# State space projections of a two-block kernel, issued as one stream with gate chunks between input and key blocks

## The chip, the cores and the metric

The kernel runs on one core of a Trainium2 chip. The metric is the device time of one execution in microseconds (us), read as the median over several executions. The core has TensorE (PE, matrix products), VectorE (DVE), ScalarE (ACT), GpSimd (POOL) and SyncE (SP, which here issues the loads of weights). Each engine works through its own instructions in order and waits for others at semaphores.

## The reference, cut to what matters

The program computes two blocks. The first is left as it is. The second has two layers; the first of them (a hybrid mixer) is left as it is as well, and the second is a state space mixer (SSD, both directions) followed by a feed-forward part. What the change touches is the mixer's input:

```
p = modulated(h) @ w_in                   # 1024 -> 2048 + (2048+1024+1024) + 32
z, xbc, dt = split(p)                     # gate z, input x / keys B / queries C, step sizes
x, B, C = silu(dwconv_centred(xbc, w, b)) # 5 taps along the tokens, per feature
dt   = softplus(dt + dt_bias)             # one bias per direction
dta  = dt * -exp(a_log)
y    = scan(x, B, C, dt, dta)  (two directions) + d_skip * x
out  = rmsnorm_by_group(y * silu(z)) @ w_out
```

There are 256 main tokens and 256 context tokens. x and B are needed for all 512 (they build the state), C and z only for the 256 main ones. `dt` is needed for all.

## The kernel before, in words

Weights arrive as 32-bit numbers and are split on chip: ACT writes the high part (`weights_hi`, line 244), DVE the remainder (`weights_lo`, line 251), and every product is three matmuls, hi by hi, hi by lo, lo by hi (`three_products`, lines 300 to 302). A unit is 512 KB of weights, 128 x 1024. There are four buffers for raw units and two for split ones, so ACT may split unit n only when PE has multiplied unit n-2, and SP loads unit n when DVE has split unit n-4.

`modulated_input` (line 2354) normalises the 512 tokens, transposes them and splits them into `work_split` and `input_split`; between its steps it splits the first two weight units (`split_first_weights`, line 2407).

`ssd_mixer` (line 3773) then runs these steps, each ended by a semaphore that all engines wait for:

- `convolution(0, 6, 2)`: six chunks of four units; a unit makes one block of 128 features for 512 tokens (24 matmuls of 512 columns). These are the four chunks of x and the two of B. The bank contents are copied into padded buffers (ACT line 3823, DVE line 3807), DVE applies tap 0 (line 3839) and taps 1 to 4 (line 3841) from the pad, and ACT applies silu with the bias (line 3814). Half of a chunk's taps come after the first half, in `half_taps`, behind a pair of weight splits.
- `convolution(6, 2, 1)`: two chunks of C for 256 tokens (24 matmuls of 256 columns per unit). It starts when the first call has ended.
- `transposes` (line 590): x and B are turned to tokens by rows, 96 transposes on PE in six batches, each batch copied out by ACT and DVE.
- `gemm_token_major` with width 32: dt for four tiles of 128 tokens, 96 matmuls whose moving side has 32 columns.
- `gemm_token_major` with width 512: z for two tiles, four chunks of four units (12 matmuls of 512 columns per unit).
- silu of z (ACT, 3927), exp of a_log (ACT, 3933), d_skip times x (DVE, 3946).
- For each direction: bias, softplus (lines 722 to 794, a chain of DVE operations 128 wide) and dta (4149), then `chunk` for the tiles of the scan, which starts on DVE at line 3965.

A `Stream` (line 938) is another way to issue products. It is already used in the first block: Python generators emit products unit by unit, in two halves, and after each half other generators may emit side work, so that it stands between the products on every engine.

## Time and profile before

| | us |
|---|---|
| median of 3 executions | 3873.2 |
| lowest and highest | 3869.24, 3876.3 |
| the profiled execution: device time | 3871.52 |
| the profiled execution: span from first to last instruction | 3869.8 |
| TensorE busy | 3338.9 |
| VectorE busy | 2084.6 |
| ScalarE busy | 1484.9 |
| GpSimd busy | 219.4 |

The profiled execution has a device time 1.7 us over its span and 1.7 us under the median. The busy time of TensorE is modelled at the ends of its matmuls, so a busy PE need not be at its peak. "Granted clock" is the share of 2.4 GHz that TensorE was given; it has two levels here, 1.00 (2.4 GHz) and 0.50 (1.2 GHz), and values between are means over a stretch.

### The profile page before, as it was taken

The page shows a single profiled execution, that of the slowest core. Times are in us where ns is not written, and L with a number is a line of the kernel's source. Part 1 is how long each engine was busy: PE and PEld are TensorE (multiplying, and loading weights), DVE is VectorE, ACT ScalarE, POOL GpSimd, SP SyncE. Part 2 cuts the span into 40 slices and gives each one's busy share as a digit, 9 for nine tenths or more (in the row PEclk, how much of TensorE's full clock was granted, in tenths as well). Part 3 has the DMA queues.
Part 4 walks back from the last instruction along what each step waited for, and adds up shares of the span by engine and source line. Part 5 has one row for each costly group of instructions (what it writes and reads, how often), then busy time and mean ns, then how long its engine had stood idle before and what let it go on. Part 6 is the DMA issues. An engine that isn't in the chain of part 4 may idle for free.

```text
span 3869.8 us, 54584 instructions
## 1 busy us (share of the span) xinstructions
PE 3338.9 (86%) x22648; PEld 2859.6 (74%) x22648; DVE 2084.6 (54%) x2794; ACT 1484.9 (38%) x2082; POOL 219.4 (6%) x268
## 2 busy tenths in 40 slices
PE   7979999797998999979698689888999796765797
PEld 6968887696887888778586588876888676565695
DVE  4546645455554664555524666754333585566554
ACT  4445444444444544344521433323222332211443
POOL 1000000000000000000001133320000000000000
PEclk9989999899898999989899889988999897877899
DMA  7745544574674554457440000012322231200363
GB/s 208 225 135 174 155 153 155 159 229 164 198 214 135 163 171 155 155 170 217 132 133 18 1 8 2 2 53 65 97 97 93 67 86 51 81 1 11 114 180 135
DMA packets 461611, 460.79 MB, mean 119 GB/s; under 512 B 18272, under 2 KB 347152, under 8 KB 461264
## 3 DMA queue, kind: packets, MB, share of 16 engines
q1 hardware_dynamic: 454720, 435.42, 36.6%
q0 software_dynamic: 6672, 22.23, 1.9%
q8 instruction: 165, 2.70, 0.3%
q14 instruction: 54, 0.44, 0.0%
HBM read 456.54 MB, written 1.05 MB: 118 GB/s over the span
## 4 chain that ended last, share of the span: by engine, by line
PE 72%; DVE 18%; ACT 5%; issue 3%; DMA 1%; POOL 0%; DVEq 0%; SPq 0%; ACTq 0%; POOLq 0%
PE banks L300 19%; PE banks L302 18%; PE banks L301 18%; DVE weights_lo L286 1%; DVE arena L3841 1%; PE banks L1260 1%; PE banks L1835 1%; PE banks L1834 1%; PE banks L4043 1%; PE banks L3458 1%; PE banks L3460 1%; PE banks L3439 1%; DVE weights_lo L251 1%; PE banks L4094 1%; DVE third_weights_split L286 1%
## 5 line engine op out<-in xcount | busy, mean ns | idle before, releaser
L286 DVE TENSOR_TENSOR weights_lo<-raw_weights,weights_hi 128x1024 fp32r<-128x1024 f32 (+2 forms) x411 | 488.6, 1196 | 439.6 <-ACT weights_hi L278 350.9
L278 ACT ACTIVATE weights_hi<-raw_weights 128x1024 fp32r<-128x1024 f32 (+2 forms) x411 | 421.7, 1035 | 540.9 <-PE banks L302 537.1
L251 DVE TENSOR_TENSOR weights_lo<-raw_weights,weights_hi 128x1024 fp32r<-128x1024 f32 x232 | 284.1, 1227 | 561.4 <-ACT weights_hi L244 373.8
L244 ACT ACTIVATE weights_hi<-raw_weights 128x1024 fp32r<-128x1024 f32 x232 | 245.2, 1059 | 661.1 <-PE banks L302 652.7
L300 PE MATMUL banks<-first_input_split,weights_hi 128*128 128x256 f32 x1320 | 380.4, 288 | 10.4 <-DVE weights_lo L286 4.8
L302 PE MATMUL banks<-first_input_split,weights_lo 128*128 128x256 f32 x1320 | 376.3, 285 | 0.0
L301 PE MATMUL banks<-first_input_split,weights_hi 128*128 128x256 f32 x1320 | 374.3, 284 | 0.0
L286 DVE TENSOR_TENSOR third_weights_split<-raw_weights,third_weights_split 128x1024 fp32r<-128x1024 f32 (+1 forms) x205 | 246.0, 1200 | 175.7 <-ACT third_weights_split L278 131.5
L300 PE MATMUL banks<-work_split,weights_hi 128*128 128x512 f32 (+1 forms) x768 | 268.1, 349 | 44.4 <-DVE weights_lo L251 25.9
L278 ACT ACTIVATE third_weights_split<-raw_weights 128x1024 fp32r<-128x1024 f32 (+1 forms) x205 | 212.0, 1034 | 216.5 <-PE banks L302 212.4
L300 PEld LDWEIGHTS banks<-first_input_split,weights_hi 128*128 128x128 f32 x1320 | 252.7, 191 | 20.1 <-DVE weights_lo L286 7.5
L301 PE MATMUL banks<-input_split,weights_hi 128*128 128x512 f32 (+1 forms) x768 | 266.7, 347 | 0.0
L302 PE MATMUL banks<-work_split,weights_lo 128*128 128x512 f32 (+1 forms) x768 | 266.4, 347 | 0.0
L301 PEld LDWEIGHTS banks<-first_input_split,weights_hi 128*128 128x128 f32 x1320 | 254.6, 193 | 1.9
L302 PEld LDWEIGHTS banks<-first_input_split,weights_lo 128*128 128x128 f32 x1320 | 251.2, 190 | 0.0
L300 PE MATMUL banks<-weights_hi,first_input_split 128*128 128x512 f32 (+1 forms) x528 | 214.3, 406 | 10.8 <-DVE weights_lo L286 8.4
L301 PE MATMUL banks<-weights_lo,first_input_split 128*128 128x512 f32 (+1 forms) x528 | 209.8, 397 | 0.0
L302 PE MATMUL banks<-weights_hi,first_input_split 128*128 128x512 f32 (+1 forms) x528 | 209.6, 397 | 0.0
L300 PE MATMUL banks<-weights_hi,work_split 128*128 128x512 f32 (+2 forms) x448 | 174.5, 390 | 28.4 <-DVEq L2333 17.2
L300 PEld LDWEIGHTS banks<-work_split,weights_hi 128*128 128x128 f32 x768 | 147.0, 191 | 67.6 <-DVEq L2333 21.3
L301 PE MATMUL banks<-weights_lo,work_split 128*128 128x512 f32 (+2 forms) x448 | 172.7, 385 | 0.0
L1260 PE MATMUL banks<-identity,arena 128*128 128x128 f32 x288 | 55.4, 359 | 125.0 <-DVE arena L1235 110.7
(598 smaller groups left out, 7295.8 us busy)
## 6 DMA issues: line engine op xcount, KB each, us to landing
raw_weights<-in_w_ffn_gu SPq DMA_DIRECT2D x176, 512.0 KB, 4.9
raw_weights<-in_w_in SPq DMA_DIRECT2D x144, 512.0 KB, 3.4
raw_weights<-in_mlp_w SPq DMA_DIRECT2D x128, 512.0 KB, 3.9
raw_weights<-in_ada_w SPq DMA_DIRECT2D x96, 512.0 KB, 4.3
raw_weights<-in_w_ffn_down SPq DMA_DIRECT2D x80, 512.0 KB, 3.8
raw_weights<-in_w_branch SPq DMA_DIRECT2D x48, 512.0 KB, 3.5
raw_weights<-in_ssd_w_in SPq DMA_DIRECT2D x48, 512.0 KB, 3.8
raw_weights<-in_w_mkv SPq DMA_DIRECT2D x32, 512.0 KB, 3.8
```

Of the source, the lines that this page charges most:

```text
L244: last = s.activation(self.w_hi[:, u % 2, :], self.raw[:, u, :], ACT.Copy)
L251: last = v.tensor_tensor(self.w_lo[:, u % 2, :], self.raw[:, u, :], self.w_hi[:, u % 2, :].bitcast(F32), ALU.subtract)
L278: last = s.activation(hi, raw, ACT.Copy)
L286: last = v.tensor_tensor(lo, raw, hi.bitcast(F32), ALU.subtract)
L300: pe.matmul(out, left_hi, right_hi, start=start, stop=False)
L301: pe.matmul(out, left_hi, right_lo, start=False, stop=False)
L302: return pe.matmul(out, left_lo, right_hi, start=False, stop=stop)
L1260: last = pe.transpose(bank(q)[:, j, :], src, c.ident[:, :])
L1834: pe.matmul(c.ps[0:4, 6, :], c.cond_split[:, k, :], hi[:, part, :], start=(k == 0), stop=False)
L1835: return pe.matmul(c.ps[0:4, 6, :], c.cond_split[:, k, :], lo[:, part, :], start=False, stop=(k == KD - 1))
L3439: last = pe.matmul(g.of_block(b, h, 256), block(g.level, b, h), block(g.inv_t, b, h), start=True, stop=True)
L3458: pe.matmul(g.of_block(b, h, P), block(g.inv, b, h), block(g.half, b, h), start=True, stop=True)
```

## The change

The projections of the mixer become one `Stream` of 17 stretches, in a class `StateSpaceInput`:

- first dt, with the weights as the stationary side: 24 matmuls of 512 columns into 32 partitions, then four transposes;
- four groups of: two pairs of x blocks, one pair of B blocks, one chunk of z (four units);
- then the two chunks of C.

A pair's banks are no longer copied to a pad. ACT writes centre tap times bank plus bias into the destination (`Identity` with scale and bias), and DVE adds the other four taps, reading the banks directly, shorter at the edges. Silu follows later on ACT, over the whole pair, then eight transposes on PE into banks 4 to 7 and two copies (ACT, DVE). This side work is emitted between half units. Silu is applied to z as it is taken from its banks. The step sizes of both directions are computed once, 256 wide, between the first stretches. d_skip times x moves from DVE to POOL. The pads and the clearing of their edges go. `modulated_input` splits the first two units of dt (128 x 64 each) in place of two whole units.

```diff
-    convolution(0, 6, 2)
-    convolution(6, 2, 1)
-    c.transposes([([xs_t[:, i + g, t // NT, t % NT * P:(t % NT + 1) * P] for g in range(4)],
-                   xs[:, t, i * P:(i + 4) * P].rearrange("p (g n) -> p g n", g=4))
-                  for i in range(0, D_IN // P, 4) for t in range(ROWS)])
...
-    c.gemm_token_major(range(ROWS), 1, column_chunks(w_in, 6144, SSD_HEADS), SSD_HEADS,
-                       *token_copies(c, dt_raw, range(ROWS), SSD_HEADS), more=True)
-    c.gemm_token_major(range(NT), 4, column_chunks(w_in, 0), BANK, *token_copies(c, z, range(NT)))
...
+        self.sizes = Stretch(token_units(w_in, 6144, SSD_HEADS), steps_times(c, whole), step_sizes,
+                             ready=lambda: self.begin())
...
+        self.stream = Stream(c, [self.sizes] + [x for i in range(4) for x in self.inputs[2 * i:2 * i + 2] + [self.keys[i], z[i]]] + self.queries)
...
+        def scalar(s, banks):
+            for n in range(blocks):
+                last = s.activation(dst(n), bank(banks, n), ACT.Identity, bias=conv_b[:, first + n:first + n + 1],
+                                    scale=taps[:, first + n, 2:3])
+            return last
+
+        def vector(v, banks, part=None):
+            if part is None:
+                order = [(tap, n) for tap in (0, 1, 3, 4) for n in range(2)]
...
+                last = v.scalar_tensor_tensor(dst(n)[:, :, to], bank(banks, n)[:, :, of], taps[:, first + n, tap:tap + 1],
+                                              dst(n)[:, :, to], ALU.mult, ALU.add)
...
-            if due is not None and u == 1 and not stretch.apart:
-                self.take(due)
+            if due is not None and u >= due.behind and not stretch.apart and self.take(due):
                 due = None
...
+    def skip(self, n):
...
+        @c.block.gpsimd
+        def _(p):
+            p.wait_ge(ch.steps_done, n)
+            for t in range(NT):
+                last = p.tensor_tensor(self.y[:, t, :].rearrange("p (h d) -> p h d", d=SSD_P),
+                                       self.xs[:, t, :].rearrange("p (h d) -> p h d", d=SSD_P),
+                                       self.parts.d_skip.unsqueeze(2).broadcast_to([P, SSD_HEADS, SSD_P]), ALU.mult)
...
+    c.ring = 2
...
-        c.softplus(raw, dt, t1, t2, t3)
```

The order on DVE shows where the taps of a pair of B and the weight splits of the gate stand. Before, in the gate's product (`L901` copies z from the banks):

```order
3827 L251 TENSOR_TENSOR weights_lo<-raw_weights,weights_hi 128x1024 [waits weights_hi_made] x4
3828 L901 COPY arena<-banks 128x512 [waits units_multiplied]
3829 L251 TENSOR_TENSOR weights_lo<-raw_weights,weights_hi 128x1024 [waits weights_hi_made] x4
3830 L901 COPY arena<-banks 128x512 [waits units_multiplied]
3831 L251 TENSOR_TENSOR weights_lo<-raw_weights,weights_hi 128x1024 [waits weights_hi_made] x4
```

Now, where the gate's first chunk but one begins (`L289` splits its units, `L3874` is the taps of the pair of B before it, `L3952` a copy of transposed x):

```order
3717 L289 TENSOR_TENSOR weights_lo<-raw_weights,weights_hi 128x1024 [waits weights_hi_made]
3718 L286 UNCONDITIONAL_BRANCH
3719 L289 TENSOR_TENSOR weights_lo<-raw_weights,weights_hi 128x1024 [waits weights_hi_made]
3720 L1060 UNCONDITIONAL_BRANCH
3721 L3874 SCALAR_TENSOR_TENSOR arena<-banks,arena 128x2x254 [waits products_taken_by_scalar,units_multiplied]
3722 L3874 SCALAR_TENSOR_TENSOR arena<-banks,arena 128x2x254
3723 L3874 SCALAR_TENSOR_TENSOR arena<-banks,arena 128x2x255 [waits convolution_taps_done] x4
3724 L3874 SCALAR_TENSOR_TENSOR arena<-banks,arena 128x2x254 [waits convolution_taps_done] x2
3725 L3949 UNCONDITIONAL_BRANCH
3726 L3952 COPY arena<-banks 128x2x256 [waits side_steps_done]
3727 L286 UNCONDITIONAL_BRANCH
3728 L289 TENSOR_TENSOR weights_lo<-raw_weights,weights_hi 128x1024 [waits weights_hi_made]
```

Eight taps and a copy now stand between the splits of the gate's second and third unit.

On PE the transposes of a pair (`L3937`) now stand inside the first unit of a gate chunk, between its two halves:

```order
14289 L303 MATMUL banks<-work_split,weights_hi 128x512
14290 L304 MATMUL banks<-input_split,weights_hi 128x512
14291 L305 MATMUL banks<-work_split,weights_lo 128x512
14292 L3931 UNCONDITIONAL_BRANCH
14293 L3937 MATMUL banks<-identity,arena 128x128 [waits side_steps_done]
14294 L3937 MATMUL banks<-identity,arena 128x128 x7
14295 L979 UNCONDITIONAL_BRANCH
14296 L303 MATMUL banks<-work_split,weights_hi 128x512
```

Before, no product stood among the 96 transposes.

## Rows read from the trace of the kernel before

**Rows 1.** The page: the span.
```profile
span 3869.8 us, 54584 instructions
```

**Rows 2.** Stretches of the mixer's input: length, busy us by engine (instructions), granted clock, DMA.
```profile
core 0: us, PE busy (x) PEld busy (x) DVE busy (x) ACT busy (x) POOL busy (x), PEclk, DMA share, GB/s
3049.00:3350.50 301.50, 239.79 (x1152) 202.51 (x1152) 184.96 (x263) 93.71 (x120) 0.00 (x0) 0.87 0.29 81
3073.00:3187.00 114.00, 110.03 (x479) 89.08 (x477) 94.15 (x131) 36.53 (x48) 0.00 (x0) 1.00 0.32 88
3187.00:3245.00 58.00, 24.94 (x192) 24.56 (x192) 40.95 (x71) 18.10 (x27) 0.00 (x0) 0.75 0.15 39
3264.00:3287.00 23.00, 20.96 (x100) 20.70 (x101) 6.41 (x6) 5.91 (x8) 0.00 (x0) 0.57 0.40 115
3333.00:3350.50 17.50, 0.00 (x0) 0.00 (x0) 10.52 (x21) 6.08 (x6) 0.00 (x0) 0.58 0.00 0
```

**Rows 3.** DVE in order of time: start, us, line, operation [idle before].
```profile
3074.96 1.28 DVE L3807 COPY arena<-banks 128x512 f32<-128x512 f32 x2
3077.20 5.77 DVE L3841 SCALAR_TENSOR_TENSOR arena<-arena 128x512 f32<-128x512 f32 x8
...
3239.61 3.63 DVE L3841 SCALAR_TENSOR_TENSOR arena<-arena 128x256 f32<-128x256 f32 x8
```

**Rows 4.** ACT in order of time; idle plus busy is one unit of PE.
```profile
3067.28 1.06 ACT L244 ACTIVATE weights_hi<-raw_weights 128x1024 fp32r<-128x1024 f32 x1 [4.38 <-PE banks L302]
...
3120.12 2.56 ACT L3814 ACTIVATE arena<-arena 128x512 f32<-128x512 f32 x4
...
3219.42 1.06 ACT L244 ACTIVATE weights_hi<-raw_weights 128x1024 fp32r<-128x1024 f32 x1 [1.82 <-PE banks L302]
...
3275.30 1.06 ACT L244 ACTIVATE weights_hi<-raw_weights 128x1024 fp32r<-128x1024 f32 x1 [4.06 <-PE banks L302]
...
3307.69 1.06 ACT L244 ACTIVATE weights_hi<-raw_weights 128x1024 fp32r<-128x1024 f32 x1 [1.69 <-PE banks L302]
```

**Rows 5.** The chain that ended last, 3010 to 3370: start, us, what.
```profile
3031.96 2.27 DVE weights_lo L251 x2
...
3049.03 0.80 PE banks L300
...
3258.16 1.98 PE banks L613 x16
...
3333.65 3.62 ACT arena L3927
...
3339.10 4.50 DVE arena L3946 x2
...
3350.51 2.36 DVE arena L3965 x2
```

**Rows 6.** DVE in order of time, between the two directions.
```profile
3448.14 1.22 DVE L4084 TENSOR_TENSOR arena<-arena,banks 128x1024 f32<-128x1024 f32 x1 [0.56 <-PE banks L4073]
...
3456.48 2.36 DVE L3965 TENSOR_TENSOR arena<-arena,small 128x1024 f32<-128x1024 f32 x2 [0.23 <-DVE small L4149]
```

**Rows 7.** Groups by line and form: operations that read banks, busy and mean ns.
```profile
L1188 DVE SCALAR_TENSOR_TENSOR arena<-banks,small,arena 128x1024 f32<-128x1024 f32 x12 | 15.4, 1280 | 0.0
...
L2872 ACT ACTIVATE spare<-banks,small 128x512 f32<-128x512 f32 x16 | 10.8, 685 | 23.5 <-DVE small L2864 23.5
```

**Rows 8.** PE in order of time, 885: the first matmul after a gap.
```profile
885.17 0.80 PE L300 MATMUL banks<-weights_hi,staged_split 128*128 128x512 f32 x1 [4.24 <-DVE arena L1933]
```

**Rows 9.** Stretches as in rows 2: after that gap, at the start of the products, inside the transposes.
```profile
885.20:888.30 3.10, 3.10 (x7) 2.46 (x8) 0.00 (x0) 0.00 (x0) 0.00 (x0) 0.50 0.75 291
...
3049.00:3052.00 3.00, 2.96 (x7) 2.39 (x8) 0.00 (x0) 0.00 (x0) 0.00 (x0) 0.50 0.00 0
3249.00:3253.00 4.00, 3.94 (x29) 3.71 (x29) 2.31 (x4) 1.91 (x4) 0.00 (x0) 0.83 0.00 0
```

**Rows 10.** All engines in order of time, 3592 to 3596: POOL beside a weight split.
```profile
3592.24 1.89 POOL L2457 TENSOR_TENSOR arena<-identity,modulations 128x1024 f32<-128x1024 f32 x1 [34.39 <-DVE arena L630]
...
3593.48 1.73 DVE L251 TENSOR_TENSOR weights_lo<-raw_weights,weights_hi 128x1024 fp32r<-128x1024 f32 x1 [1.50 <-ACT work_split L246]
3595.47 1.21 DVE L251 TENSOR_TENSOR weights_lo<-raw_weights,weights_hi 128x1024 fp32r<-128x1024 f32 x1
```

More of the change, by code:

```diff
@@ L997, in run @@
             yield
-        if due is not None:
-            self.take(due)
+        while due is not None and not self.take(due):
+            yield
         if due_apart is not None:
             self.take_apart(due_apart)
+        self.ended = True
     def begin(self, stretch):
@@ L1038, in take, with _ @@
     def take(self, stretch):
[L1039 to L1049 removed]
+        c, part = self.c, stretch.part
+        stretch.part += 1
+        ends = stretch.part == stretch.parts
+        stretch.emitted = ends
+        if part == 0:
+            @c.block.scalar
+            def _(s):
+                s.wait_ge(c.multiplied, stretch.multiplied)
+                last = stretch.take_scalar(s, stretch.banks) if stretch.take_scalar else None
+                if last is None:
+                    s.sem_inc(c.taken_by_scalar, 1)
+                else:
+                    last.then_inc(c.taken_by_scalar, 1)
         @c.block.vector
@@ L1055, in _ @@
                 v.wait_ge(c.taken_by_scalar, stretch.taken)
-            last = stretch.take_vector(v, stretch.banks) if stretch.take_vector else None
-            if last is None:
+            which = (part,) if stretch.parts > 1 else ()
+            last = stretch.take_vector(v, stretch.banks, *which) if stretch.take_vector else None
+            if not ends:
+                assert last is None
+            elif last is None:
                 v.sem_inc(c.taken_by_vector, 1)
@@ L3743, in __init__ @@
         self.c = c
-        self.pads = [cols(c.work, 4096, 4, 2, SEQ + 4), cols(c.par, 1024, 4, 2, SEQ + 4)]
         self.taps = cols(c.par, 0, 32, 5)
@@ L3755, in __init__, with blocks_times, product @@
         c.load(self.d_skip, a["ssd_d_2"][0, :].partition_broadcast(P))
-    def clear_edges(self, ends):
-        c, n = self.c, self.c.steps
+def blocks_times(c, x):
+    x_hi, x_lo = x
+    def product(pe, banks, u, part, hi, lo):
+        for k in range(4 * part, 4 * part + 4):
+            last = c.three_products(pe, c.ps[:, banks + u, :], hi[:, k, :], lo[:, k, :], x_hi[:, k, :], x_lo[:, k, :],
+                                    k == 0, k == KD - 1)
+        return last
+    return product
@@ new lines, in _, with step_sizes @@
+            p.wait_ge(ch.steps_done, n)
[3 more added lines that the diff above has]
+                                       self.parts.d_skip.unsqueeze(2).broadcast_to([P, SSD_HEADS, SSD_P]), ALU.mult)
+            last.then_inc(c.skip_made, 1)
+    def step_sizes(self):
+        c, ch, raw, (t1, t2, t3) = self.c, self.c.steps_of_size, self.raw, self.temps
+        decay_rate = self.parts.decay_rate
+        while not self.sizes_turned:
+            yield
+        turned = self.sizes_turned
@@ L3880, in ssd_mixer, with _ @@
-    y = cols(w, 4096, NT, D_IN)
+            s.wait_ge(ch.steps_done, ch.steps)
+            s.activation(decay_rate, decay_rate, ACT.Exp).then_inc(ch.steps_done, 1)
+        @c.block.vector
+        def _(v):
+            v.wait_ge(*turned)
+            v.wait_ge(ch.steps_done, ch.steps)
+            for d in range(2):
+                last = v.tensor_tensor(raw[:, d], self.dt_raw, self.parts.dt_bias[:, d:d + 1, :].broadcast_to(
+                    [P, ROWS, SSD_HEADS]), ALU.add)
+            last.then_inc(ch.steps_done, 1)
@@ new lines, in step_sizes, with _ @@
+        ch.steps += 2
+        @c.block.scalar
+        def _(s):
+            s.wait_ge(ch.steps_done, ch.steps)
+            s.activation(t1, raw, ACT.Abs).then_inc(ch.steps_done, 1)
+        ch.steps += 1
+        @c.block.scalar
+        def _(s):
+            s.wait_ge(ch.steps_done, ch.steps)
+            s.activation(t2, t1, ACT.Exp, scale=-1.0).then_inc(ch.steps_done, 1)
+        ch.steps += 1
+        yield
+        yield from half_log1p(ch, t2, self.dt, t1, t3)
+        yield
+        @c.block.vector
@@ new lines, in step_sizes, with _, run @@
+        ch.steps += 1
+        @c.block.vector
+        def _(v):
+            v.wait_ge(ch.steps_done, ch.steps)
+            for d in range(2):
+                last = v.tensor_tensor(self.dta[:, d], self.dt[:, d], decay_rate[:, d:d + 1, :].broadcast_to(
+                    [P, ROWS, SSD_HEADS]), ALU.mult)
+            last.then_inc(ch.steps_done, 1)
+        ch.steps += 1
+    def run(self):
+        c = self.c
+        beside = [self.step_sizes(), self.rows()]
+        for _ in itertools.chain(self.stream.run(), itertools.repeat(None)):
+            beside = [side for side in beside if next(side, True) is None]
+            if self.stream.ended and not beside:
+                break
+        c.chunks = c.units_split // UNITS
+        assert c.chunks * UNITS == c.units_split
+        skip, last = 1, c.taken
+        @c.block.vector
+        def _(v):
+            v.wait_ge(c.skip_made, skip)
+            v.wait_ge(c.taken_by_scalar, last)
+            v.wait_ge(c.taken_by_vector, last)
+        joined(c, [c.side, c.steps_of_size])
@@ L3881, in ssd_mixer @@
+def ssd_mixer(c, a, out, parts, inputs):
+    ps, small, w = c.ps, c.small, c.work
+    xs, b_tok, b_t, c_t, z, y = inputs.xs, inputs.b_tok, inputs.b_t, inputs.c_t, inputs.z, inputs.y
+    c.loaded()
+    inputs.run()
     state = cols(w, 8192, SSD_HEADS, SSD_P)
```

329 lines of the change are left out of this document (176 added, 153 removed).

## The prediction

> **What bounds the kernel now.** I read the page first, then the stretches of the mixer's input, then the chain of waits, and last DVE and ACT in order of time. The mixer's input runs from the first product at 3049.03 to the scan's first operation at 3350.51 [rows 5], 301.5 us of a span of 3869.8 [rows 1, 2]. PE is busy for 239.8 of them, DVE for 185.0, ACT for 93.7 [rows 2]. So no engine is the bound of the whole; the question is which stretch waits for what.
>
> - 3073 to 3187, the wide convolution: PE is busy 110.0 of 114 us at full clock, though DVE works 94.2 of them [rows 2]. PE bounds it.
> - 3187 to 3245: PE 24.9 of 58 us, DVE 41.0 [rows 2]. The first convolution must end (taps, silu) before the second starts, and again before the transposes.
> - the transposes wait for copies and go in batches of 1.98 us for 16 [rows 5].
> - 3264 to 3287, dt: PE is busy but slow, at a clock of 0.57; a unit of 24 matmuls of 32 columns takes 4.06 + 1.06 = 5.12 us [rows 2, 4].
> - 3333 to 3350.5: PE does nothing; ACT's silu of z (3.62), DVE's skip products (4.50) and the softplus stand in one chain [rows 2, 5].
> - between the two directions DVE goes from 3448.14 + 1.22 to 3456.48, 7.1 us of softplus, with the scan waiting [rows 6].
>
> **The change part by part.** First the work that PE must do, at full clock, by the unit times of rows 4 (idle plus busy of ACT between two units):
> - wide blocks, 24 units of 4.38 + 1.06 = 5.44: 130.6 us, as before.
> - z, 16 units of 1.69 + 1.06 = 2.75: 44.0, as before.
> - C, 8 units of 1.82 + 1.06 = 2.88: 23.0, as before.
> - dt: 24 matmuls of 512 columns in all, as many as one wide unit: 5.4 in place of four units of 5.12. I add 0.9 for the first wide unit, which is split only when PE has multiplied the third small one (ACT 1.06, DVE 1.14 after it, with 1.36 us of PE to cover).
> - 96 transposes at 1.98/16 = 0.124 [rows 5]: 11.9, and 0.5 for the four of dt.
> With that 0.9 PE's part is 216.3 us.
>
> Next the waits that the order of DVE makes. A pair's take is: ACT two Identity of 512, by the bank-reading row of 685 ns [rows 7] some 1.4 us; DVE eight taps. The operation "bank and SBUF into SBUF" at 512 is not in the trace; from SBUF eight take 5.77 [rows 3], and at 1024 one that reads banks takes 1280 ns [rows 7], which is no more per element. I take 5.8, with 5.0 below (half of 1.28 each) and 11.5 above (twice). Count from E, when PE ends the pair. ACT splits the next unit (E + 1.1), takes the pair (E + 2.5); DVE ends its split at E + 2.4, its taps at E + 8.4, a copy of turned rows at E + 9.0 (1.28 for two [rows 3]), and the following split at E + 10.2. Where the next stretch is a wide pair, PE needs that unit at E + 5.44 + 1.0 + 5.44 = E + 11.9: covered, 1.7 us to spare. Where it is a gate chunk, PE needs its third unit at E + 2.75 + 1.0 + 2.75 = E + 6.5 and gets it at E + 10.2: 3.7 us of wait, once in each of four chunks, 14.8 us. ACT's silu of a pair waits for the taps (E + 8.4) and ends before the next split is due, so it costs nothing; the table load after dt's exp falls there as well.
>
> The step sizes stand between the first stretches: 19 DVE operations. One direction, 128 wide, takes 7.1 us now [rows 6], so both at once cost between 7 and 14; I take 9, since the elements double and the fixed part doesn't. Followed through the queue, with the silu and two table loads on ACT behind them, they make PE wait 2.4 us for the first gate unit and lengthen the wait at its third from 3.7 to 5.1: 3.8 more.
>
> The skip products run on POOL, which has nothing else. 1024 elements take 1.89 us there [rows 10], so two of 2048 take some 8 us; they start when the last x pair is turned, and over 35 us (two gate units, C and the tail) stand behind that. They are hidden. But while POOL worked, a weight split took 1.73 us in place of 1.21 [rows 10]. Three gate or query splits can meet it: 1 us of PE. The Trainium skill, "GPSIMD Engine Reference", section Specifications, says that GpSimd shares its SBUF interfaces with VectorE and that DVE instructions with two SBUF inputs contend. By that rule the splits and copies of step sizes meet it and the taps, which read one input from the banks, don't. The trace agrees for the split.
>
> The clock. A gap of 4.24 us [rows 8] was followed by 3.1 us at 0.50, that is 1.2 GHz [rows 9]: about 1.6 us lost. The products' own start had 3 us at 0.50 [rows 9], and that comes again with dt at the start: 1.9 us. Each of the five waits above may do the same; between 0 and 3.4 us each, I take 2: 10 us.
> The transposes now stand among the products. The Trainium skill, "TensorE: Matmul & The Clock Gate", section Part 4: PE-mode transpose, says that they don't count as PE being busy for the clock. Here a stretch inside the 96 transposes rose to a mean of 0.83 [rows 9], with nothing else on PE, so the trace speaks against it. By the rule the clock could fall at each of twelve turns of 1 us; the sum goes by the row, with no cost.
>
> The tail, from the last product of C: ACT takes four blocks of 256 (1.7), DVE 16 taps of 256 at 3.63/8 (7.3) [rows 3], silu 1.1, the join 0.4: 10.5 us. It stands where 17.5 us stood [rows 2]. The taps of the first C chunk hide beside the products of the second: a part of four taps (1.8) and a split (1.14) fit a unit of 2.88 to within 0.1.
>
> Sum: 216.3 + 14.8 + 3.8 + 1.0 + 1.9 + 10 + 10.5 = 258.3 us from the first product to the scan, in place of 301.5: 43.2 less. The start is earlier: DVE's two splits of 2.27 us in the chain [rows 5] become two of 64 elements, 0.5: 1.8 less. The second direction's softplus goes: 7.1 us less, of which a wait of 0.3 stays: 6.8. Together 51.8 us. Clearing the pads was on POOL beside other work: nothing. The profiled execution took 3871.5 us (1.7 under the median), so 3819.7; against the median 3821. I say 3820.
>
> **The rivals.**
> - The waits at the gate chunks are hidden or don't cool the clock. The clock stays up where a gap is short, and the taps may take 5.0. Without the 10 us of clock and with 1 us less at each chunk: 3807. For it: the gaps are forecast near 4 us, no more. Against: the gap of 4.24 did cool it.
> - More is late than I followed: the clock stays at 0.50 for twice as long after each gap (another 8 us), a split of the pair stretches slips past its 1.7 us of room at half of the eight places (4 times 1.5, and their clock): 3836. For it: in a pair DVE has no more than 1.7 us, and the operations' waits on ACT are many. Against: DVE has 94.2 of 114 us already and PE still runs [rows 2], and after the change DVE has fewer operations per pair, since the pad copies (1.28) and tap 0 are gone.
> - A general starvation, such as side steps that hold PE's queue at the transposes: the gain halves, 3847.
> - Slower: a tap that reads a bank costs twice the one from SBUF. Each take grows by 5.8 us: in eight pairs 5.8 - 1.7 = 4.1 and 2 of clock, 49; at four gate chunks 23; in the C chunks and the tail 5 + 7: 84 us against a gain of 51, so 3905. It turns to a loss from about 1.2 us a tap. Against it stands the row of 1280 ns for 1024 elements from a bank [rows 7].
> - The change doesn't overlap as it says: PE's own order shows that products of one stretch stand directly behind those of the one before, with no join between; only a value of a semaphore set too high could hold them. That would be near 3870.
>
> **How the numbers follow.** Forecast 3820 (its own range 3812 to 3829) 0.46; hidden waits, 3807, 0.20; more late, 3836, 0.20; halved, 3847, 0.08; no overlap 0.02; slower 0.04. The range of 3802 to 3842 leaves out the halved gain, the no-overlap case and the slower one with the ends of the others. 0.2% is 8 us, about what can be told from no change. Faster 0.94, same 0.02, slower 0.04.
>
> **What would show it.** Right: PE's first 512-column products of dt at about 3047 of the span and the scan at about 3305; wide units 5.44 us apart; a wait of PE of 3.5 to 4 us for `weights_lo` at each gate chunk's third unit, with the clock at 0.50 behind it; transposes in eights of 1.0 us; eight taps in 5.8 us; DVE going from one direction to the next without softplus. Wrong: PE waiting at wide pairs, taps of over 0.9 us, PE held by the transposes, or a tail over 15 us. The forecast falls if the gate's waits are absent or occur at every stretch.

## The result, and the profile after

| | before | after |
|---|---|---|
| median, us | 3873.39 | 3813.0 |
| lowest and highest, us | 3869.24, 3876.3 | 3808.31, 3819.4 |
| executions | 4 | 4 |
| profiled execution: device time, us | 3871.52 | 3808.31 |
| its span, us | 3869.8 | 3806.6 |
| first product to the scan, us | 301.5 | 250.9 |

The ratio of the two is 0.9846, with a 95% interval from 0.9826 to 0.9866: 60 us less, 52 to 67. The forecast was 3820, 53 less.

The page of the changed kernel, its span and busy times (against [rows 1]):

```profile
span 3806.6 us, 54217 instructions
PE 3313.6 (87%) x22580; PEld 2834.5 (74%) x22580; DVE 2045.7 (54%) x2724; ACT 1489.8 (39%) x2080; POOL 227.8 (6%) x266
```

The same stretches as windows, with the columns of [rows 2]: the whole mixer's input, its first 5 us, the wait in the first group's gate chunk and the work behind it, two x pairs with a key pair, the second half of the last gate chunk with C (its wait included), the tail, and the first two steps of the scan:

```profile
3045.34:3296.20 250.86, 223.54 (x1084) 183.87 (x1084) 152.94 (x210) 100.11 (x120) 9.10 (x2) 0.96 0.38 105
3045.34:3050.34 5.00, 5.00 (x12) 2.05 (x13) 0.23 (x1) 0.26 (x1) 0.00 (x0) 0.50 0.07 15
...
3096.60:3105.00 8.40, 4.23 (x12) 3.31 (x12) 5.30 (x7) 1.06 (x1) 0.00 (x0) 0.80 0.37 100
3105.00:3148.00 43.00, 43.00 (x198) 35.38 (x196) 24.58 (x31) 17.68 (x20) 0.00 (x0) 1.00 0.37 103
...
3247.70:3286.30 38.60, 34.30 (x249) 32.32 (x248) 26.50 (x34) 18.31 (x22) 9.10 (x2) 0.96 0.49 137
3286.30:3296.20 9.90, 0.00 (x0) 0.00 (x0) 6.33 (x16) 4.05 (x7) 0.00 (x0) 0.65 0.00 0
3296.20:3316.40 20.20, 15.44 (x62) 13.30 (x62) 16.29 (x15) 2.01 (x5) 0.00 (x0) 0.75 0.00 1
```

Where [rows 2] had PE busy for 239.8 of 301.5 us, it is now busy for 223.5 of 250.9. Inside wide pairs and transposes (3105 to 3148) it never stops: 43.00 of 43.00 us, with DVE at 24.6. What is left of its waits stands in three rows of the view of waits, for PE in this stretch (what waited, who released it: us in all, times, longest):

```profile
PE banks L303 <- DVE weights_lo L289: 17.4, 7, 4.2
PE banks L303 <- DVEq L2346: 13.1, 1, 13.1
PE banks L4113 <- DVEq L2346: 10.0, 1, 10.0
```

The second row is the wait before the first product and lies outside the stretch. The first row has seven waits for a split: 1.09 for the first wide unit, 1.09 for the first gate unit, 4.17, 3.38, 3.38 and 3.38 at the third unit of the four gate chunks, and 0.89 before C. The third is the tail.

**One gate chunk.** PE in order of time around the third unit of the first chunk, and DVE before it:

```profile
3096.26 0.39 PE L305 MATMUL banks<-weights_hi,input_split 128*128 128x512 f32 x1
3100.82 0.50 PE L303 MATMUL banks<-weights_hi,work_split 128*128 128x512 f32 x1 [4.17 <-DVE weights_lo L289]
...
3101.62 0.63 PE L303 MATMUL banks<-weights_hi,work_split 128*128 128x512 f32 x1
...
3105.03 0.39 PE L305 MATMUL banks<-weights_hi,input_split 128*128 128x512 f32 x1
```
```profile
3091.94 1.22 DVE L289 TENSOR_TENSOR weights_lo<-raw_weights,weights_hi 128x1024 fp32r<-128x1024 f32 x1
3093.07 0.19 DVE L4029 TENSOR_SCALAR arena<-arena 128x64 f32<-128x64 f32 x1
3093.29 0.50 DVE L4036 TENSOR_TENSOR arena<-arena 128x128 f32<-128x128 f32 x2
3093.71 5.33 DVE L3874 SCALAR_TENSOR_TENSOR arena<-banks,arena 128x508 f32<-128x508 f32 x8
3098.95 0.68 DVE L3952 COPY arena<-banks 128x512 f32<-128x512 f32 x1
3099.55 2.35 DVE L289 TENSOR_TENSOR weights_lo<-raw_weights,weights_hi 128x1024 fp32r<-128x1024 f32 x2
```

ACT had rounded the unit by 3095.1, but its split (3099.55) stands in DVE's queue behind the eight taps of the key pair and a copy. PE's products then last 0.63 us each in place of 0.39 until 3105.0: the granted clock is 0.50 there. Gaps of 4.17, 3.38 and 3.38 were followed by such a fall (3101.6, 3152.8 and 3251.8, each 3.4 us long); the gap of 3.38 at 3198.66 was not. The ends of the four gaps lie 50.61, 50.62 and 49.05 us apart, with the same work between, and a fall in the first two of these stretches alone; so a fall costs 1.57 us, the difference.

**The last gate chunk**, on DVE and then on POOL in order of time (POOL's two operations as lines of their own):

```profile
3252.07 3.54 DVE L289 TENSOR_TENSOR weights_lo<-raw_weights,weights_hi 128x1024 fp32r<-128x1024 f32 x1 [1.02 <-ACT weights_hi L281]
...
3257.82 2.36 DVE L289 TENSOR_TENSOR weights_lo<-raw_weights,weights_hi 128x1024 fp32r<-128x1024 f32 x1 [1.61 <-ACT weights_hi L281]
3260.53 1.23 DVE L289 TENSOR_TENSOR weights_lo<-raw_weights,weights_hi 128x1024 fp32r<-128x1024 f32 x1 [0.35 <-ACT weights_hi L281]
```
```profile
3250.00 4.53 POOL L3970 TENSOR_TENSOR arena<-arena 128x2048 f32<-128x2048 f32 x1 [577.97 <-DVE arena L3952]
3254.49 4.61 POOL L3970 TENSOR_TENSOR arena<-arena 128x2048 f32<-128x2048 f32 x1
```

A split that takes 1.23 us alone took 3.54 and 2.36 beside POOL's two skip products. The Trainium skill ("GPSIMD Engine Reference", section Specifications) says that the two engines contend where a DVE instruction has two SBUF inputs. The trace agrees, and more strongly than [rows 10] had it (1.73 us). The first of the two fell where DVE had time; only the second reached PE, with 0.89 us. The rows also show how a split is held. POOL's first operation ends at 3254.53 and the split beside it at 3255.61; POOL's second ends at 3259.10 and the split beside it at 3260.18. Both splits end 1.08 us after the POOL operation that was running when they began, nearly the time of a whole split, so they got next to nothing done until it was over.

**The rest of the span.** The start, from the chain of waits:

```profile
3029.68 0.27 DVE weights_lo L289 x2
...
3045.34 0.63 PE banks L303
```

It is 15.66 us from the start of the splits to the first product, against 17.07 in [rows 5]: 1.4 less. Between the directions, DVE in order of time:

```profile
3391.67 1.22 DVE L4238 TENSOR_TENSOR arena<-arena,banks 128x1024 f32<-128x1024 f32 x1 [0.56 <-PE banks L4227]
3393.30 2.36 DVE L4119 TENSOR_TENSOR arena<-arena 128x1024 f32<-128x1024 f32 x2 [0.41 <-DVE arena L4238]
```

A gap of 0.4 us stands where [rows 6] had 7.1. What follows takes 413.30 us, before 413.32. The first direction without that gap takes 96.7 us (3296.20 to 3392.89), before 98.9 (3350.51 to 3449.36), though its work is the same. In its first two steps PE ran the same 62 matmuls in 20.20 us at a clock of 0.75 (last window above), in the kernel before, in 21.90 us at 0.64:

```profile
3350.50:3372.40 21.90, 17.12 (x62) 14.49 (x62) 16.30 (x15) 0.85 (x4) 0.00 (x0) 0.64 0.00 1
```

So the difference of the spans, 63.2 us, is 50.6 in the products, 6.7 between the directions, 2.2 in the first direction, 1.4 at the start, and 2.3 before that (the splits of the start stand at 3031.96 and 3029.68), where both kernels execute the same. Two of these parts are no larger than what executions of one and the same program differ by. In the seven kernels below, whose program differs from the changed kernel's in the stretch alone, the splits of the start stand between 3027 and 3036, the scan takes 97.0 to 99.3 us up to the second direction, and what follows takes 416.7 to 418.5, where the two profiled executions compared here took 413.3. So the 2.2 and 2.3 us can't be put down to the change.

### The profile page after: what moved, and what is told of

The parts are those of the page before. It is cut to its first block, busy times and chain, and to the rows that moved or that the text cites. A ratio compares the mean times of both kernels' runs of the same rounds, so it can differ in the third digit from the quotient of the medians.

```text
span 3806.6 us, 54217 instructions
## 1 busy us (share of the span) xinstructions
PE 3313.6 (87%) x22580; PEld 2834.5 (74%) x22580; DVE 2045.7 (54%) x2724; ACT 1489.8 (39%) x2080; POOL 227.8 (6%) x266
## 4 chain that ended last, share of the span: by engine, by line
PE 73%; DVE 17%; ACT 5%; issue 3%; DMA 1%; POOL 0%; DVEq 0%; SPq 0%; ACTq 0%; POOLq 0%
PE banks L303 19%; PE banks L304 19%; PE banks L305 19%; DVE weights_lo L289 2%; PE banks L1273 1%; PE banks L1848 1%; PE banks L1847 1%; DVE arena L3874 1%; PE banks L3474 1%; PE banks L3476 1%; PE banks L4197 1%; PE banks L3455 1%; ACT weights_hi L281 1%; DVE third_weights_split L289 1%; PE banks L1870 1%
## 5 line engine op out<-in xcount | busy, mean ns | idle before, releaser
L289 DVE TENSOR_TENSOR weights_lo<-raw_weights,weights_hi 128x1024 fp32r<-128x1024 f32 (+1 forms) x463 | 551.3, 1198 | 526.6 <-ACT weights_hi L281 439.1
L281 ACT ACTIVATE weights_hi<-raw_weights 128x1024 fp32r<-128x1024 f32 (+1 forms) x463 | 473.3, 1030 | 652.3 <-PE banks L305 649.6
L254 DVE TENSOR_TENSOR weights_lo<-raw_weights,weights_hi 128x1024 fp32r<-128x1024 f32 x180 | 220.8, 1228 | 471.4 <-ACT weights_hi L247 283.8
L247 ACT ACTIVATE weights_hi<-raw_weights 128x1024 fp32r<-128x1024 f32 x180 | 190.4, 1059 | 515.4 <-PE banks L305 509.9
L289 DVE TENSOR_TENSOR third_weights_split<-raw_weights,third_weights_split 128x1024 fp32r<-128x1024 f32 (+1 forms) x205 | 246.0, 1200 | 174.8 <-ACT third_weights_split L281 130.6
L303 PE MATMUL banks<-work_split,weights_hi 128*128 128x512 f32 (+2 forms) x776 | 270.9, 349 | 22.0 <-DVEq L2346 20.0
L304 PE MATMUL banks<-input_split,weights_hi 128*128 128x512 f32 (+2 forms) x776 | 269.6, 347 | 0.0
L305 PE MATMUL banks<-work_split,weights_lo 128*128 128x512 f32 (+2 forms) x776 | 269.4, 347 | 0.0
L303 PE MATMUL banks<-weights_hi,work_split 128*128 128x512 f32 (+1 forms) x416 | 164.3, 395 | 39.0 <-DVEq L2346 16.3
L303 PEld LDWEIGHTS banks<-work_split,weights_hi 128*128 128x128 f32 (+1 forms) x776 | 146.9, 189 | 44.9 <-issue 14.4
L304 PE MATMUL banks<-weights_lo,work_split 128*128 128x512 f32 (+1 forms) x416 | 161.6, 388 | 0.0
```

The lines of the kernel that those rows point to most:

```text
L247: last = s.activation(self.w_hi[:, u % 2, :], self.raw[:, u, :], ACT.Copy)
L254: last = v.tensor_tensor(self.w_lo[:, u % 2, :], self.raw[:, u, :], self.w_hi[:, u % 2, :].bitcast(F32), ALU.subtract)
L281: last = s.activation(hi, raw, ACT.Copy)
L289: last = v.tensor_tensor(lo, raw, hi.bitcast(F32), ALU.subtract)
L303: pe.matmul(out, left_hi, right_hi, start=start, stop=False)
L304: pe.matmul(out, left_hi, right_lo, start=False, stop=False)
```

## The experiments

Of each kernel the median and its ratio to the kernel before are given, and from its profile the stretch from the first product to the scan, 250.9 us in the changed kernel. The stretch is the finer measure: in the profiled executions of the kernels below the first product stands between 3042.8 and 3051.4 us, though the program ahead of it is the same, so the totals carry some us that the edits did not make. By the ratios alone only the joined pairs, the gate last and the combined kernel stand clear of the changed kernel (0.9826 to 0.9866); of the other four the intervals overlap with its own, and their reading rests on the stretch of one profiled execution each. All edits are made on the changed kernel.

**Key pairs' taps in parts.** Each key pair is taken in four parts, one after each split, so that the taps no longer stand in a lump ahead of the gate's third unit.

```diff
-        self.keys = [convolved(at["b"] + i, lambda n, i=i: self.b_t[:, i + n]) for i in range(0, SSD_G, 2)]
+        self.keys = [convolved(at["b"] + i, lambda n, i=i: self.b_t[:, i + n], 4) for i in range(0, SSD_G, 2)]
```

> The eight taps of each B pair are given out in four parts of two, one behind each unit of the gate chunk; all else as in the changed kernel. Theory (DVE's order makes PE wait): the four gaps of PE at the gate's third unit (4.17, 3.38, 3.39, 3.38 us in the changed kernel) go, save about 1 us of the first, and with them the three falls of the clock behind them (about 1.6 us each). The projections' stretch goes from 250.9 to about 233 us and the time from 3813 to about 3795. Rival (DVE or ACT is late at the gate for another cause, the splits, the copies or the order of ACT): the gaps spread over the units and the time stays above 3808.

Measured: 3809.13 us (3802.08 to 3820.06), ratio 0.9838 (0.9816 to 0.986); stretch 242.0, so 9 less. PE's waits:

```profile
PE banks L4113 <- DVEq L2346: 10.0, 1, 10.0
PE banks L303 <- DVE weights_lo L289: 5.7, 5, 3.1
PE banks L303 <- DVE arena L3874: 5.5, 4, 1.4
```

The waits at the third gate unit are gone in the first three chunks, and with them two of the three falls of the clock: the lump of taps was their cause. The median of 3809 is what the rival named (over 3808), but the rival's cause isn't there: the waits that are left have other origins. Less came back than expected, for two reasons that the rows show. Four new waits of 1.4 us have the taps themselves as releaser (L3874): the pair behind the gate chunk uses the key pair's banks, and those come free only with the last part, which now stands behind the split of the fourth unit. And the skip products, starting at 3234.0, met two splits with no time to spare:

```profile
3234.14 4.57 DVE L289 TENSOR_TENSOR weights_lo<-raw_weights,weights_hi 128x1024 fp32r<-128x1024 f32 x1 [0.21 <-ACT weights_hi L281]
3238.64 1.39 DVE L3874 SCALAR_TENSOR_TENSOR arena<-banks,arena 128x510 f32<-128x510 f32 x2
3239.95 3.32 DVE L289 TENSOR_TENSOR weights_lo<-raw_weights,weights_hi 128x1024 fp32r<-128x1024 f32 x1
```

PE waited 3.1 us for the first of them, at the third unit of the last gate chunk, and the one fall of the clock stands there. The two taps between the splits, which read one input from the banks, took their usual time (1.39 us; 1.40 at 3231.93, before POOL began).

**The gate last.** The order of the stretches is changed: no gate chunk between the groups, all four after C.

```diff
-... [x for i in range(4) for x in self.inputs[2 * i:2 * i + 2] + [self.keys[i], z[i]]] + self.queries)
+... [x for i in range(4) for x in self.inputs[2 * i:2 * i + 2] + [self.keys[i]]] + self.queries + z)
```

> The four gate chunks are moved from between the pairs to the end of the stream, behind C; all else as in the changed kernel. Theory: pairs back to back keep 2 us of room on DVE, so nothing is lost there; the taps of the last C chunk come in four parts beside gate units, and the tail after the last product shrinks from 9.9 to about 2.5 us (one silu of 1024 columns, the join). With the four gaps and their cold clock gone the time is about 3788 (25 us less). Rival (the gate chunks are what gives DVE the time to catch up, so dealing them out is what pays): without them PE waits for weight splits at the pairs, and the time is 3813 or more.

Measured: 3796.02 us (3792.3 to 3800.02), ratio 0.9797 (0.978 to 0.9815); stretch 230.1, so 20.9 less. PE's waits and the window of the stretch:

```profile
PE banks L303 <- DVE weights_lo L289: 6.2, 4, 3.1
PE banks L303 <- DVE arena L3874: 3.1, 2, 1.6
PE banks L4113 <- DVEq L2346: 1.9, 1, 1.9
```
```profile
3046.16:3276.23 230.07, 218.93 (x1084) 180.97 (x1084) 153.38 (x211) 100.63 (x120) 9.10 (x2) 0.99 0.42 115
```

The tail is 1.9 us in place of 9.9, since the last taps, silu and join now lie beside gate products; the waits for splits are 6.2 in place of 17.4; and PE needs 4.6 us less for the same 1084 matmuls, as the clock falls once (after a wait of 3.1 at 3200.2) and not three times, and is up 3.1 us after the first product and not 5.1. Dealing the gate out among the groups, which the change does, costs some 20 us against putting it last. It falls short of the expected 25 by a wait of 3.1 at the third unit of C and the fall at it: the last key pair's lump now stands ahead of C's short units, as it stood ahead of the gate's. Two waits for the taps of the C chunks, 1.5 and 1.6, are new as well.

**Step sizes late.** The softplus and what follows it run after the products, for both directions at once.

```diff
-        beside = [self.step_sizes(), self.rows()]
+        beside = [self.rows()]
...
+        for _ in self.step_sizes():
+            pass
```

> The step sizes of both directions (still computed once, 256 wide) are issued after the stream in place of between its first stretches. Theory (they hide beside the products): the tail grows by their whole chain, about 9.8 us of DVE and 2.5 of ACT, and the first group gets back 1.9 us of PE's waits: +10 us, 3823. Rival (their place costs as much as it saves, by blocking DVE and ACT in the first group and cooling the clock): within 3 us of 3813.

Measured: 3822.79 us (3820.93 to 3824.83), ratio 0.9865 (0.9848 to 0.9881); stretch 261.2, so 10.2 more. The wait ahead of the scan grows by 11.0, those for splits fall from 17.4 to 16.8:

```profile
PE banks L4115 <- DVEq L2346: 21.0, 1, 21.0
PE banks L303 <- DVE weights_lo L289: 16.8, 7, 3.4
```

Without the small operations on DVE the wait of 1.09 at the first gate unit is gone and the one at the third is 3.38 like the others, not 4.17: 1.9 us less. The waits beside POOL's skip products were 0.64 and 1.55 in place of 0.89, 1.3 more. So beside the products the step sizes cost PE 1.9 us, in the open 11.

**Skip products on DVE.** They leave POOL and stand behind the last silu, as before the change.

```diff
-            if i == len(self.inputs) - 1:
-                self.skip(ch.steps)
...
+            for t in range(NT):
+                v.tensor_tensor(self.y[:, t, :]..., self.xs[:, t, :]..., self.parts.d_skip..., ALU.mult)
```

> The products of x with d_skip are done on DVE after its last taps, as the kernel before does, and not on POOL beside the stream. Theory: two operations of 2.25 us stand in the tail, 1.1 of them beside ACT's last silu, and DVE's weight splits are no longer stretched (3.54 and 2.36 us in place of 1.22 at 3252 and 3258), which gives PE back 0.9 us: +2.5 us, 3815. Rival (the contention of POOL with DVE costs more than the products are worth): 3 us or more faster than the changed kernel, 3810 or less.

Measured: 3818.3 us (3815.36 to 3822.99), ratio 0.9854 (0.9836 to 0.9871); stretch 253.4, so 2.5 more. The total is 5 us over the changed kernel's, and the intervals of the two ratios overlap; the profile shows the parts:

```profile
PE banks L303 <- DVE weights_lo L289: 16.5, 6, 4.1
PE banks L4117 <- DVEq L2346: 13.8, 1, 13.8
```

The wait of 0.89 us before C is gone with POOL's work, and the tail is 3.7 longer: DVE takes 4.49 us for the two products, part of it beside the last silu. POOL is worth its place, though it holds a split to nearly three times its time.

**dt by narrow units.** dt's products again give tokens by heads, four tokens' blocks of 32 columns each, in place of heads by tokens with 512 columns and four turns.

```diff
-        return c.three_products(pe, c.ps[0:SSD_HEADS, banks, :], hi[:, part, :], lo[:, part, :], x_hi[:, k, :],
-                                x_lo[:, k, :], k == 0, k == KD - 1)
+        for t in range(ROWS):
+            tokens = slice(t * P, (t + 1) * P)
+            last = c.three_products(pe, c.ps[:, 4 + t, 0:SSD_HEADS], x_hi[:, k, tokens], x_lo[:, k, tokens],
+                                    hi[:, part, :], lo[:, part, :], k == 0, k == KD - 1)
```

> The product of dt is done as the kernel before does it: tokens as the stationary side, 96 matmuls of 32 columns into four banks, no transposes; its place at the head of the stream and all else as in the changed kernel. Theory (the narrow moving side is what cost 20.5 us before): four units of 5.12 us in place of 8.0 from the stream's start to the end of dt (3045.34 to 3053.38), so +12 us, and the clock stays at 0.50 through dt and into the first wide unit, another 1 to 2 us: 3826. Rival (the 5.12 us came from the clock alone, which was at 0.50 there for another reason): at the full clock 24 matmuls of 32 columns take 24 x 0.11 = 2.7 us a unit, so 10.8 in all: +3 us, 3816.

Measured: 3828.42 us (3826.1 to 3834.63), ratio 0.9878 (0.9854 to 0.9903); stretch 264.6 (the scan's first operation stands at 3310.23), so 13.7 more. The windows of dt with the first products behind it, and of dt alone:

```profile
3045.63:3069.00 23.37, 23.37 (x103) 22.79 (x104) 2.90 (x4) 2.62 (x4) 0.00 (x0) 0.50 0.24 68
3045.63:3066.10 20.47, 20.47 (x96) 20.47 (x97) 1.68 (x3) 1.57 (x3) 0.00 (x0) 0.50 0.24 67
```

PE shows as busy through all 23.37 us, yet the granted clock stays at 0.50 and rises only when wide products come (cold until 3071.1, in the changed kernel until 3050.4). Two splits of these units stand at 3051.32 and 3056.44 on DVE, 5.12 us apart, the same as in [rows 4]. The four units take 20.5 us, where dt in the wide form takes 8.0 from the start (3045.34 to 3053.38), and the first 5.0 us of wide products behind them run at 0.50 as well, half of which is lost: 12.4 and 2.5, less some 1.1 in small waits and the four turns of dt. The theory holds; of its two terms the first (12) was right, the second (1 to 2) a little small. The form of the product is worth 14 us, nearly a quarter of the change's gain. The second window shows where the time of dt goes: the loads of the stationary side are busy for all of it, 97 of them, 0.21 us each, one for every product of 32 columns. The rival, 0.11 us a product at the full clock, was not met, as the clock never rose; that price itself is on record in the kernel before, whose first narrow products start 0.11 us apart while the clock is still at 1.00 (3266.04 to 3267.39).

**Joined pairs.** A pair of blocks is taken before the next stretch begins, as the kernel before does it at each convolution; all else is as changed.

```diff
             if u == 0:
+                while due is not None and stretch.parts > 0 and c.ring == 2:
+                    if self.take(due):
+                        due = None
                 self.begin(stretch)
...
-        free = c.taken if stretch.whole else c.taken - 1
+        free = c.taken if stretch.whole or c.ring == 2 else c.taken - 1
```

> Every stretch of the stream begins only when the products of the one before are taken from their banks, so taking no longer stands beside products; all work and its order else are as in the changed kernel. Theory (the overlap of taking with products is what the stream pays): each of 12 pairs then costs PE 1.4 (ACT) and 5.3 (taps), the first C chunk 8, each gate chunk 1.1, less the four gate gaps of 3.4 to 4.2 which go, plus about 1.6 us of cold clock at each of some 13 places: about +105 us, 3918, slower than the kernel before. Rival (the gain is from dt, the tail and the softplus, and the overlap is worth little, as the kernel before overlaps within its chunks as well): +30 us or less, 3843.

Measured: 3936.89 us (two executions), ratio 1.0154 (1.0124 to 1.0184): slower than the kernel before. The stretch is 371.4, so 120.5 more. PE's waits and one of them as a window, the second from the clock's fall on:

```profile
PE banks L303 <- DVE arena L3877: 101.6, 13, 8.9
...
PE banks L4116 <- DVEq L2349: 10.0, 1, 10.0
PE banks L303 <- ACT arena L3837: 8.4, 4, 2.3
```
```profile
3093.47:3105.00 11.53, 4.10 (x10) 3.23 (x11) 8.38 (x15) 3.16 (x5) 0.00 (x0) 0.70 0.17 45
3098.10:3105.00 6.90, 4.10 (x10) 3.23 (x11) 4.25 (x10) 1.06 (x1) 0.00 (x0) 0.51 0.02 6
```

Thirteen waits for taps, 7.4 to 8.9 us each, and a fall of the clock at every one. Behind the wait shown PE has 4.1 us of work at 0.50; over the thirteen it is 2.9 to 6.2 us, 59.5 in all, half of which, 29.7, is lost, where the changed kernel loses 5.1 at its three. Against the changed kernel PE's waits in the stretch grow by 94.5 us (111.9 from 17.4) and its busy time by 26.0 (249.6 from 223.5): together the 120.5. The direction was the one expected and the size too small. The expectation's own terms add up to 99 and not 105: 78.5 for the waits and 20.8 for the clock. A pair's take was put at 6.7 us and cost 7.4 or more, and a fall was put at 1.6 us and cost 2.3 on average. The new order is a gain only with its overlap: the overlap is worth 124 us, twice the gain of the change. No run puts the pads back, so what reading the banks directly is worth within this stream is not shown.

**Combined.** From what the above showed: gate last; the taps of the last key pair alone in four parts; the skip products in sixteen POOL operations of 256 columns.

```diff
+        self.keys = [convolved(at["b"] + i, ..., 4 if i == 6 else 1) for i in range(0, SSD_G, 2)]
+        self.stream = Stream(c, ... self.inputs[2 * i:2 * i + 2] + [self.keys[i]]] + self.queries + z)
...
+                for h in range(0, SSD_HEADS, 4):
+                    at = slice(h * SSD_P, (h + 4) * SSD_P)
```

> The gate chunks at the end of the stream, the taps of the last B pair in four parts beside the first C chunk, and the skip products on POOL in 16 operations of 256 columns in place of two of 2048. Theory (a long POOL operation holds DVE's weight splits, a short one does so for less): no split takes over 2.2 us, the gap of 3.1 us before C goes to 1.4, and the stream from the first product to the scan takes 226 us in place of 230.1 with the gate last alone: 3792. Rival (what holds a split is POOL being busy, whatever the size of its operations): 16 operations take some 14 us and hold five splits by 0.6 us or more each, and the stream stays at 230 us or goes over it.

Measured: 3792.8 us (3787.53 to 3795.3), ratio 0.9778 (0.9754 to 0.9801): 20 us under the changed kernel. Stretch 226.7. PE's waits, and POOL with one of the splits beside it:

```profile
PE banks L303 <- DVE arena L3875: 4.4, 3, 1.6
PE banks L303 <- DVE weights_lo L289: 2.2, 2, 1.1
PE banks L4117 <- DVEq L2346: 1.9, 1, 1.9
```
```profile
3204.34 13.12 POOL L3973 TENSOR_TENSOR arena<-arena 128x256 f32<-128x256 f32 x16 [526.04 <-DVE arena L3953]
```
```profile
3214.16 1.70 DVE L289 TENSOR_TENSOR weights_lo<-raw_weights,weights_hi 128x1024 fp32r<-128x1024 f32 x1 [0.27 <-ACT weights_hi L281]
```

The wait of 3.1 at C's third unit is gone (one of 1.3 for the last part of the taps stands before the second C chunk), and once up after the start the clock does not fall before the scan. In pieces, POOL takes 13.1 us in place of 9.1, and no split beside it takes more than 1.70. The rival is ruled out, and the times of the single operations say why: as in the changed kernel, each of the four splits beside POOL ends 1.08 us after the end of the one POOL operation beside its start, and a piece of 0.61 us is soon over. The price is POOL's: twelve pieces take 0.61 us and four, each begun while a split ran, 1.59. The stretch is 3.4 us under that of the gate last; by their totals the two cannot be told apart (intervals of 0.9754 to 0.9801 and 0.978 to 0.9815).

## Why the prediction was right, and where its sizes were off

The mechanism was the one forecast: PE's own work bounds the stretch, with one wait at the third unit of each gate chunk, the clock down behind it, and a tail. Term by term, from the first product to the scan:

| term | forecast | profile after |
|---|---|---|
| PE's work at full clock | 215.4 | 216.4 |
| waits at gate units | 18.6 | 15.4 |
| first wide unit | 0.9 | 1.1 |
| POOL's contention | 1.0 | 0.9 |
| clock at the start | 1.9 | 2.5 |
| clock after gaps | 10.0 | 4.7 |
| tail | 10.5 | 9.9 |
| sum | 258.3 | 250.9 |

(PE's work is what the rest leaves; the clock at the start is half of 5.06 us at 0.50.)

- **PE's work** held to 1 us in sum, though not in each part: a turn of eight transposes takes 0.79 us at full clock (3242.59 to 3243.39) and not 0.99, so all twelve cost 9.5 us in place of 11.9, and what the rest leaves hides some 3 us that no row here takes apart. No clock fell at the transposes; in 3105 to 3148 it is 1.00 throughout. The rule of the Trainium skill weighed in the prediction ("TensorE: Matmul & The Clock Gate", Part 4) is that these don't count as busy for the clock. The turns can't test it, since they are of 0.8 us and pauses of 0.9 and 1.1 us had no fall either. The kernel before speaks against it: after a pause of 11.15 us nothing ran on PE but transposes from 3245.03 on, and the granted clock went from 0.50 to 1.00 at 3250.33.
- **Waits at the gate** were 3.4 and not 3.7 us, since eight taps took 5.33 and not 5.8: `banks` as a source costs no more per element than SBUF, as the row of 1280 ns said [rows 7]. The step sizes added 1.9 us (1.09 at the first gate unit, 0.79 at the third) where 3.8 were expected. Their operations sum to 8.7 us on DVE, near the 9 that I took; it was my count through the queues that left DVE too little room. The experiment with parts shows what makes the gate's waits, the one with the gate last what they and the tail cost.
- **The clock after gaps** was the term that was mis-sized most: five falls at 2 us were forecast, three came at 1.57. I knew one gap of 4.24 with a fall [rows 8, 9] and took every gap as such. Of the gaps here those of 1.1 and 0.9 had none, and of three gaps of 3.4 one had none; so a gap of that size falls on either side. The trace of before could have told part of this. In the same stretch it has a gap of 2.77 us with no fall (the clock stays at 1.00 until 3236.67) and one of 3.89 with a fall at 3267.39, and the sum looked at neither:

```profile
3227.85 0.39 PE L300 MATMUL banks<-work_split,weights_hi 128*128 128x256 f32 x1 [2.77 <-DVE weights_lo L251]
3266.04 0.26 PE L300 MATMUL banks<-weights_hi,work_split 128*128 128x32 f32 x1 [3.89 <-DVE weights_lo L251]
```

- **The tail** (9.9 for 10.5) and **the end of the first direction** (6.7 for 6.8) held. The start gave 1.4 in place of 1.8: the two splits shrank by 2.0 us, but 0.6 of PE's issue stands behind them.
- **Not foreseen**: the 2.2 us in the first direction. The first steps ran at a clock of 0.75 and not 0.64. The shorter pause of PE ahead of them (10.0 us, where 17.5 had no work) isn't the reason: with the gate last and in the combined kernel that pause is 1.89 us in both, and from the scan to the second direction it is 98.9 us in the one (3276.12 to 3375.04) and 97.3 in the other (3278.04 to 3375.34), 97.1 in the changed kernel. With the key pairs' taps in parts the pause is 10.0 us as in the changed kernel, and the direction takes 99.0 (3284.68 to 3383.71). What decides between 97 and 99 stays open; it varies among kernels whose program is the same there.
- **POOL's contention** was right in size by luck. A split beside it took up to 3.54 us, not the 1.73 of [rows 10]; only the place, beside gate units with DVE idle, hid it. What the forecast lacked is that a split stands still until the POOL operation beside it ends, so that its delay goes with what is left of that operation. In the experiment with parts the same two POOL operations cost a wait of 3.1 us and a fall of the clock.

Of the rivals, the hidden waits (3807) was the nearer one on the clock and wrong on the waits, which all came; the wide pairs never waited, against the rival of more being late (whose own terms, 8, 4 times 1.5 and four falls at 2, add up to 22 us and so to 3842, not 3836); and a tap from a bank took 0.67 us, far from the 1.2 at which the change would have lost. The rival of no overlap at 3870 had the wrong price as well: without it, the changed order costs 3937, since it has thirteen joins where the kernel before had few.

The profiled execution took 3808.3 us, 11.4 under the sum of 3819.7: 7.4 of it are in the stretch, 2.2 in the first direction, 2.3 in the part ahead of the mixer, and 0.5 went the other way at the start and between the directions. The median lies 4.7 over that execution and so 7 under the forecast. The 2.2 and 2.3 are the parts that vary between executions: by what the change itself did, the sum of 3819.7 was 6.9 too high.

## What to carry to other kernels

When stretches of one engine's work are put in a stream, look at each boundary for what the second engine still owes from the stretch before, and whether the next stretch's units are long enough to cover it: taps in a lump are hidden beside wide units of 5.4 us and exposed beside short ones of 2.75. Short units that need little of the helper belong at the end, where they cover a tail, and not between, where they ask for splits faster than the helper's backlog lets them. Cutting a backlog into parts has its price where a later stretch waits for the buffer that the last part frees: 1.4 us a time here, against 3.4 and now and then a fall of the clock for the lump. And where an engine beside holds the helper for as long as one of its operations lasts, as POOL does here, give it its work in small pieces.

## What the runs showed of the hardware

- A DVE operation with two SBUF inputs of 1024 elements took 1.23 us alone and 3.54, 4.57, 3.32 and 2.36 us beside a POOL operation of 2048 elements. Beside POOL operations of 256 it took 1.28 to 1.70, while POOL's own work went from 9.1 to 13.1 us. In the stretches measured here and in [rows 10] sixteen splits began while POOL was at work, and each ended 1.08 us after the end of the POOL operation beside its start, whether that had 256, 1024 or 2048 elements. POOL is held in turn: an operation of 2048 took 3.62 us when no split was running at its start, and 4.53 to 4.61 when one was. Copies out of the banks and taps that read one input from the banks kept their times beside POOL (0.68 and 0.73 us each).
- Whether the granted clock falls after a pause of PE is not settled by the pause's length: of three pauses of 3.38 us in one execution two were followed by 3.4 us at 0.50, one by none. With the step sizes late there were four pauses of 3.38; three had a fall. Shorter ones had a fall too, 3.10 us with the taps in parts and 3.11 with the gate last. After eight pauses of 7.4 us PE had between 3.1 and 6.2 us of its work at half speed.
- PE at products of 32 columns, each with its own load of the stationary side, showed as busy for 20.47 of 20.47 us with the clock at 0.50 all through; the wide products behind them had it up after 5.0 us.
